# TensorE multiplies ones into an unused PSUM bank at eleven places of a two-block network kernel

## The chip, the cores and the metric

One NeuronCore of a Trainium2 chip runs the kernel. Its engines are TensorE (PE, with its weight loads listed as PEld), VectorE (DVE), ScalarE (ACT), GpSimd (POOL) and SyncE (SP), which here issues most of the DMAs. The metric is the time of one execution on the device in microseconds (us); lower is better.

## What is computed

256 tokens of width 1024 in float32 go through two blocks. The first has a depthwise convolution, an attention with a forget gate and 32 experts, of which each token takes 4. The second has two layers with a windowed attention and a retention in both directions, then a dense feed-forward in the first layer and 8 experts, 2 for each token, in the second. What matters here are the norms and the two routings, since the change stands around them:

```python
def rms_norm(x, g):
    y = xf * lax.rsqrt(jnp.mean(xf * xf, axis=-1, keepdims=True) + RMS_EPS)
    return (y * g)
def layer_norm_2(x, g, b):
    mu = jnp.mean(xf, axis=-1, keepdims=True)
    var = jnp.mean(jnp.square(xf - mu), axis=-1, keepdims=True)
    return ((xf - mu) * lax.rsqrt(var + LN_EPS)) * g + b

# routing of block 1 (block 2: 8 experts, top 2)
logits = (hf @ w_router + b_router)
top_v, top_e = lax.top_k(logits, TOP_K)
gates = jax.nn.softmax(top_v, axis=-1)
# each expert
hc = xi @ w1[e] + b1[e]
hm = (u + 1.0) * (g * jax.nn.sigmoid(SWIGLU_ALPHA * g))
y += gate * (hm @ w2[e] + b2[e])

# between the blocks and inside the second
x = rms_norm(x, final_g); x = layer_norm_2(x, ln_emb_g, ln_emb_b)
for layer in range(2):
    x = layer_norm_2(ALPHA * x + hybrid_mixer(x), ln1_g[layer], ln1_b[layer])
    x = layer_norm_2(ALPHA * x + ffn(x), ln2_g[layer], ln2_b[layer])
```

## The kernel before

Activations lie with the features on the partitions: X and H are 128 x 8 x 256 (feature within a tile, tile, token). Each engine runs a program written out by hand, in that order, and the engines wait for each other by counted semaphores; nothing is scheduled by a planner. Weights come by DMAs that SyncE issues in the order of use into a ring in SBUF; a slot is refilled when PE has used it.

**Sums over features.** Features lie on partitions, so a norm's sums are products with ONES, a 128x128 tile of ones, as the stationary side: each brings the sum over 128 features to all partitions. `squares` (L880) does it for the norm ahead of the first experts, `shift_sum` (L740) and `moments` (L748) for the layer norms, L1040 for the rms norm between the blocks. The layer norms first subtract an estimate of the mean (`shift_sum` on two tiles) and then take the sum and the sum of squares of the shifted values. DVE turns the sums into a factor (L1709 to L1752: a subtraction, ACT's square root, a reciprocal, the multiplication), ACT applies gain and bias pair of tiles by pair of tiles (L1476, L1395), and PE's next products wait for each pair.

**First products behind a norm.** `first_jobs` (L683) runs the first two weight slots of a stage pair by pair, with weights and activations in two float32r parts (WHI_D, WLO_D, XHI, XLO). POOL makes WLO_D (L400) for each slot from what ACT rounded (L396).

**Routing** (`route`, once for each expert stage). PE computes the logits (L903, moving part 32 or 8 columns), turns the tokens (L896), sums the mask of chosen experts (L909 to L912) and, in the first, turns the gates (L918). DVE computes the table of chunks from them; two small products (L922) bring it into a row. Then PE gathers the first chunk's tokens with a one-hot tile (L956 with 64 columns in the first stage, L1052 with 512 in the second), adds the bias products (L932, first stage only) and reads the number of chunks into a register (L936). The loop over chunks of 64 slots starts with L992 in the first stage and L1094 in the second. In each chunk PE also turns tiles and gathers for the next chunk (L1003, L956).

**The end.** PE turns the normed output (L1329), ACT and DVE copy it and SyncE stores it.

The line numbers here and in the prediction are those of this kernel.

Of the kernel before, what the change touches and what calls it, by code (L numbers as in the profile page):

```python
# [28 lines left out]
P = 128  # L29
# [110 lines left out]
def build_two_blocks(nc, A, out):  # L140
# [3 lines left out]
    with ctx:  # L144
        sems = {}

        def sem(name):
            if name not in sems:
                sems[name] = ctx.enter_context(nc.semaphore(name))
            return sems[name]  # L150
# [30 lines left out]
        ONES = sb("ONES", [P, P])  # L181
# [128 lines left out]
        def ps(b, n=512, p0=0, p1=P, c0=0):  # L310
            return PS[p0:p1, b, c0:c0 + n]
# [307 lines left out]
        def _(pe):  # L619
            norm = [0]  # L620

            def bank_free(job):
                if job >= 2:
                    e, c = job_evac[job - 2]
                    pe.wait_ge(sem("evac_" + e), c)
# [111 lines left out]
            def shift_sum(src, b):  # L737

                for k in range(2):
                    mm = pe.matmul(ps(b, T), ONES[:, :], src[:, k, :], start=(k == 0), stop=(k == 1))  # L740
                mm.then_inc(sem("norm_sum"), 1)

            def moments(src, squares, p, first, last, b1, b2):


                def total(bank, c0, x):
                    for k in (2 * p, 2 * p + 1):
                        mm = pe.matmul(ps(bank, T, c0=c0), ONES[:, :], x[:, k, :],  # L748
                                       start=(first and k == 2 * p), stop=(last and k == 2 * p + 1))
                    if last:  # L750
                        mm.then_inc(sem("norm_sum"), 1)

                norm[0] += 1
                if not last:
                    pe.wait_ge(sem("norm_in"), norm[0])
                total(b1, 0, src)
                pe.wait_ge(sem("norm_in"), norm[0])
                total(b2, T, squares)
# [116 lines left out]
            def squares(s):  # L875

                norm[0] += 1
                pe.wait_ge(sem("norm_in"), norm[0])
                for k in (2 * s, 2 * s + 1):
                    mm = pe.matmul(ps(4, T), ONES[:, :], SQV[:, k, :], start=(k == 0), stop=(k == KT - 1))  # L880
                mm.then_inc(sem("norm_sum"), 1)

            for s in range(4):
                feature_job(lins["w_out"], s, z(GC, GC + 8))
                if s:
                    squares(s - 1)
            squares(3)

            def route(m, x, wr, gather):

# [24 lines left out]
                if m is m1:  # L915
                    pe.wait_ge(sem("route_gates"), 1)
                    for a in range(2):
                        tr = pe.transpose(ps(1, P, c0=a * P), GATE4[:, a, :, :].rearrange("p r e -> p (r e)"), IDENT[:, :])  # L918
                    tr.then_inc(sem("gates_turned"), 1)
                pe.wait_ge(sem("route_table_cols"), m.nth)  # L920
                for j in range(2):
                    mm = pe.matmul(ps(3, P, 0, 1, 256 + j * P), TCOL[:, j:j + 1], IDENT[:, :], start=True, stop=True)  # L922
# [16 lines left out]
            def scatter_last(tag):  # L939


                for j in range(2):
                    for h in range(2):
                        c = (2 + j) * P
                        mm = pe.matmul(ps(4 + h, T, c0=j * T), YS1[64 * h:64 * h + 64, c:c + P], GT[64 * h:64 * h + 64, :],
                                       start=True, stop=True)
                mm.then_inc(sem(tag + "_scattered"), 1)

            def experts1():
# [81 lines left out]
                pe.wait_ge(sem("m1_ys_copied"), count + 1)  # L1031
                scatter(count, 0)
                scatter_last("m1")
                pe.wait_ge(sem("xw_ready"), 1)
                shift_sum(XW[:, 0:2, :], 1)
                for i, p in enumerate((0, 2, 1)):
                    moments(XW, XWSQ, p, i == 0, False, 3, 1)
                pe.wait_ge(sem("x_squared"), 1)
# [2 lines left out]
                mm.then_inc(sem("norm_sum"), 1)  # L1041
                pe.wait_ge(sem("xw_shifted"), 1)
                moments(XW, XWSQ, 3, False, True, 3, 1)

            def experts2():

# [100 lines left out]
                scatter_last("m2")  # L1147
                pe.wait_ge(sem("x_added"), 3)
                shift_sum(X, 3)
                for i, p in enumerate((0, 2, 1, 3)):  # L1150
                    if i == 3:
                        pe.wait_ge(sem("xw_shifted"), 2)
                    moments(X, H, p, i == 0, i == 3, 2, 3)
# [3 lines left out]
            def mixer2(l):  # L1157
# [112 lines left out]
                moments(X, H, 2, False, False, 5, 4)  # L1270
                pe.wait_ge(sem("evac_dve"), job_evac[lin.job0 + 3][1])
                moments(X, H, 3, False, True, 5, 4)

            mixer2(0)
            first_jobs(lins["ffn1"])
# [43 lines left out]
            for p in range(4):  # L1319
                if p == 3:  # L1320
                    pe.wait_ge(sem("x_added"), 2)
                moments(X, H, p, p == 0, p == 3, 5, 4)
            mixer2(1)
            experts2()
            for k in range(KT):
                if k % 2 == 0:
                    pe.wait_ge(sem("stream_x"), 16 + k // 2 + 1)
                for a in range(2):
                    tr = pe.transpose(ps(4 + 2 * a + k // 4, P, c0=(k % 4) * P), X[:, k, a * P:(a + 1) * P], IDENT[:, :])  # L1329
                    if k % 4 == 3:  # L1330
                        tr.then_inc(sem("out_turned"), 1)
# [1017 lines left out]
```

## Time and profile before

| | us |
|---|---|
| median of 3 runs (2408.94 to 2410.05) | 2409.09 |
| the profiled execution | 2402.67 |
| its span, first to last instruction | 2400.7 |
| PE busy in it | 2273.2 (95%) |
| VectorE, ScalarE, GpSimd busy | 735.9, 621.7, 385.2 |
| mean granted TensorE clock | 0.976 of full speed |

The stages by time in the span: norms, projections, convolution and attention of the first block until about 277; first routing until 306; 33 chunks of the first experts until 1270; the norms between the blocks until 1299; the first mixer until 1518; the dense feed-forward until 1724; the second mixer until 1948; second routing until 1972; 11 chunks of the second experts until 2375; the last norm and the output until 2400.7.

How to read it. Busy time counts pipelined products up to a modelled end, so that 95% does not say that PE runs at its peak. The granted clock is given as a share of 2.4 GHz: 1.00 is 2.4, 0.50 is 1.2 GHz, and a value between is the mean of a stretch in which it changed. A matmul on float32 data stands as two records in the trace. In a row of the timeline, the bracket at the end gives the idle time ahead and what ended it.

### The profile page before, as it was taken

Reading aid. Unit: us, or ns where it says so; the run is one execution under the profiler, and the core shown is the slowest. Engines: PE = TensorE matmul, PEld = TensorE weight load, DVE = VectorE, ACT = ScalarE, POOL = GpSimd, SP = SyncE. Lnnn points to the kernel's source line nnn. Section 1 sums busy time; section 2 is a strip of 40 time slices with the busy share of each in tenths; the row PEclk is TensorE's granted clock in tenths of the full one; section 3 lists DMA queues with packets and bytes.
Section 4 is the critical chain, followed back from the end, with each engine's and each line's share of the span. In section 5 each row is a group of like instructions: output and inputs, shape, how many; then the busy total and the mean of one; then the engine's idle time right before and its main releaser. Section 6 shows DMA issues by size and latency. Waiting matters only on the chain.

```text
span 2400.7 us, 34716 instructions
## 1 busy us (share of the span) xinstructions
PE 2273.2 (95%) x13090; PEld 1407.5 (59%) x13091; DVE 735.9 (31%) x1369; ACT 621.7 (26%) x901; POOL 385.2 (16%) x355
## 2 busy tenths in 40 slices
PE   5999899999999999999997999999999989999897
PEld 4887744444444444444446988899898863333333
DVE  6854322222222222222235234312314341111013
ACT  1143111111111111111214761443368011111111
POOL 1000000000000000000004741688486000000000
PEclk8999899999999999999998999999999989999999
DMA  9962389999999999989993433565454366999651
GB/s 371 370 233 101 95 341 418 418 418 417 418 417 418 417 418 417 418 341 414 418 393 106 158 106 105 163 190 180 119 176 124 122 249 260 362 405 396 278 234 72
DMA packets 226472, 688.61 MB, mean 287 GB/s; under 512 B 31386, under 2 KB 120418, under 8 KB 190562
## 3 DMA queue, kind: packets, MB, share of 16 engines
q1 hardware_dynamic: 221776, 685.82, 74.5%
q10 hardware_dynamic: 4626, 1.81, 0.3%
q8 instruction: 50, 0.82, 0.1%
q14 instruction: 20, 0.16, 0.0%
HBM read 686.53 MB, written 1.05 MB: 286 GB/s over the span
## 4 chain that ended last, share of the span: by engine, by line
PE 73%; DMA 10%; SPq 8%; DVE 4%; issue 1%; ACT 1%; ACTq 1%; POOL 0%; DVEq 0%; POOLq 0%
PE PS L992 16%; PE PS L651 12%; PE PS L662 11%; DMA RAW<-in_w_exp_in 9%; PE PS L1094 7%; SPq L453 6%; PE PS L1105 4%; PE PS L956 4%; PE PS L1287 3%; PE PS L975 2%; PE PS L706 1%; PE PS L748 1%; SPq L475 1%; PE PS L1003 1%; PE PS L1052 1%
## 5 line engine op out<-in xcount | busy, mean ns | idle before, releaser
L992 PE MATMUL PS<-RAW,Z 128*64 128x512 f32 x3168 | 713.7, 597 | 23.2 <-DMA RAW<-in_w_exp_in 23.2
L400 POOL TENSOR_TENSOR WLO_D<-W,WHI_D 128x512 fp32r<-128x512 f32 x284 | 361.8, 1310 | 1193.1 <-ACT WHI_D L396 1164.3
L992 PEld LDWEIGHTS PS<-RAW,Z 128*64 128x64 f32 x3168 | 213.7, 137 | 454.4 <-issue 376.7
L1094 PE MATMUL PS<-W,Z 128*64 128x512 f32 (+1 forms) x1056 | 212.8, 558 | 11.3 <-DMA W<-in_moe_w 10.6
L662 PE MATMUL PS<-Z,W 128*128 128x256 f32 x768 | 172.2, 385 | 2.1 <-DVE Z L1900 1.5
L396 ACT ACTIVATE WHI_D<-W 128x2048 fp32r<-128x2048 f32 x71 | 135.3, 1908 | 119.4 <-DMA W<-in_ffn_w 47.6
L1094 PEld LDWEIGHTS PS<-W,Z 128*64 128x64 f32 x1056 | 75.1, 137 | 149.1 <-issue 128.2
L662 PEld LDWEIGHTS PS<-Z,W 128*128 128x128 f32 x768 | 147.6, 193 | 25.2 <-DVE Z L1900 1.9
L956 PE MATMUL PS<-Z 128*128 128x64 f32 x1088 | 128.6, 278 | 0.0
L956 PEld LDWEIGHTS PS<-Z 128*128 128x128 f32 x1088 | 127.4, 196 | 0.3 <-issue 0.3
L2021 DVE TENSOR_TENSOR Z<-Z,PS 128x1024 f32<-128x1024 f32 x66 | 80.4, 1218 | 125.9 <-PE PS L975 125.9
L662 PE MATMUL PS<-H,W 128*128 128x256 f32 x512 | 116.1, 388 | 2.4 <-ACT Z L1432 2.4
L1515 ACT ACTIVATE Z<-PS 128x512 f32<-128x512 f32 x33 | 19.7, 597 | 367.1 <-PE PS L992 367.1
L651 PE MATMUL PS<-XHI,WHI_D 128*128 128x256 f32 x784 | 111.7, 285 | 1.4 <-POOL WLO_D L400 1.4
L1105 PE MATMUL PS<-W,Z 128*64 128x512 f32 x484 | 111.1, 599 | 0.0
L651 PE MATMUL PS<-XHI,WLO_D 128*128 128x256 f32 x784 | 110.1, 283 | 0.0
L651 PE MATMUL PS<-XLO,WHI_D 128*128 128x256 f32 x784 | 110.0, 283 | 0.0
L2047 DVE COPY Z<-PS 128x512 f32<-128x512 f32 x33 | 22.8, 692 | 280.0 <-PE PS L992 280.0
L662 PEld LDWEIGHTS PS<-H,W 128*128 128x128 f32 x512 | 98.8, 195 | 16.6 <-issue 2.9
L651 PEld LDWEIGHTS PS<-XHI,WHI_D 128*128 128x128 f32 x784 | 100.7, 191 | 3.1 <-POOL WLO_D L400 2.0
L651 PEld LDWEIGHTS PS<-XLO,WHI_D 128*128 128x128 f32 x784 | 101.1, 192 | 0.0
L651 PEld LDWEIGHTS PS<-XHI,WLO_D 128*128 128x128 f32 x784 | 101.1, 192 | 0.0
(384 smaller groups left out, 2333.8 us busy)
## 6 DMA issues: line engine op xcount, KB each, us to landing
RAW<-in_w_exp_in SPq DMA_DIRECT2D x256, 1024.0 KB, 19.3
RAW<-in_w_exp_out SPq DMA_DIRECT2D x128, 1024.0 KB, 21.8
W<-in_moe_w SPq DMA_DIRECT2D x128, 704.0 KB, 15.8
W<-in_w_in SPq DMA_DIRECT2D x52, 1024.0 KB, 5.9
W<-in_moe_w SPq DMA_DIRECT2D x40, 1024.0 KB, 16.1
W<-in_ffn_w SPq DMA_DIRECT2D x33, 1024.0 KB, 5.3
W<-in_w_ada SPq DMA_DIRECT2D x24, 1024.0 KB, 14.0
W<-in_w_out SPq DMA_DIRECT2D x12, 1024.0 KB, 5.1
```

Of the source, the lines that this page charges most:

```text
L396: eng.activation(hi, raw, ACT.Copy).then_inc(sem("dense_hi"), 1)
L400: i = eng.tensor_tensor(lo[:, c:c + 512], raw[:, c:c + 512], hi[:, c:c + 512].bitcast(F32), ALU.subtract)
L453: sp.dma_start(dst, src).then_inc(sem(f"raw{s}"), 16)
L651: mm = pe.matmul(ps(job % 2, T, c0=j * T), w[:, k, c:c + P], xp[:, k, :], start=(i == k == 0), stop=(i == 2 and k == KT - 1))
L662: mm = pe.matmul(ps(job % 2, T, c0=j * T), w[:, k, c:c + P], x[:, k, :], start=(k == 0), stop=(k == nk - 1))
L956: mm = pe.matmul(ps(2, HALF, c0=k * HALF), HT[:, a, k * P:(k + 1) * P], PICK[:, a, 0:HALF], start=(a == 0), stop=(a == 1))
L975: mm = pe.matmul(ps(6 + h, T, c0=j * T), YS1[64 * h:64 * h + 64, c:c + P], GT[64 * h:64 * h + 64, :], start=True, stop=True)
L992: mm = pe.matmul(ps(bank, 512, 64 * h, 64 * h + 64), x, w[:, c:c + 512], start=first, stop=final, skip_group_check=True)
L1094: mm = pe.matmul(o if b < 2 else o.rearrange("p (i n) -> p i n", i=2), X1[:, s, :], rhs, start=(s == 0), stop=(s == 7), skip_group_check=True)
L1105: mm = pe.matmul(ps(3, 512, 64 * h, 64 * h + 64), x, second2(j)[:, c:c + 512], start=(i == j == 0), stop=(j == 5), skip_group_check=True)
L1287: mm = pe.matmul(ps(j // 2, T, c0=(j % 2) * T), w[a][:, i, j * P:(j + 1) * P], x[:, i, :], start=(s == n == i == 0 and j % 2 == 0), stop=( ...
L2021: dve.tensor_tensor(o, o, PS[:, 6:8, :].rearrange("p h (k t) -> p h k t", k=2), ALU.add)\
```

## The change

A helper `busy(n, b)` is added to PE's program. It issues n float32 products with ONES as stationary and ONES, read four times, as 512 moving columns, into PSUM bank 2 or 0, a bank that nobody reads before it is written anew. The products wait for nothing and raise no semaphore. It is called at eleven places: behind the squares of the norm ahead of the first routing (5); in `route` behind the transposes and ahead of the wait for the table (2, in both routings); behind the last scatter of the first experts (5), behind `shift_sum` (2) and behind the moments (6) between the blocks; behind `shift_sum` of the last norm (2); behind the moments at the end of each mixer (5, twice) and of the feed-forward (5); and ahead of the output's transposes (5). No other instruction is changed.

```diff
+            def busy(n, b=2):
+                for _ in range(n):
+                    pe.matmul(ps(b).rearrange("p (a n) -> p a n", a=4), ONES[:, :],
+                              ONES[:, :].unsqueeze(1).broadcast_to([P, 4, P]), start=True, stop=True)
...
             squares(3)
+            busy(5)
...
                     tr.then_inc(sem("gates_turned"), 1)
+                busy(2)
                 pe.wait_ge(sem("route_table_cols"), m.nth)
...
                 scatter_last("m1")
+                busy(5)
                 pe.wait_ge(sem("xw_ready"), 1)
                 shift_sum(XW[:, 0:2, :], 1)
+                busy(2)
                 for i, p in enumerate((0, 2, 1)):
...
                 moments(XW, XWSQ, 3, False, True, 3, 1)
+                busy(6)
...
                 shift_sum(X, 3)
+                busy(2, 0)
...
                 moments(X, H, 3, False, True, 5, 4)
+                busy(5)
...
                 moments(X, H, p, p == 0, p == 3, 5, 4)
+            busy(5)
             mixer2(1)
             experts2()
+            busy(5, 0)
             for k in range(KT):
```

PE's order at the first routing before: the squares, the logits with the router's weights WR, the turned tokens, the mask sums, the gates, the table, the gather.

```order
L880 MATMUL PS<-SQ,ONES 128x256 x4
L903 MATMUL PS<-WR,H 128x32 x16
L896 MATMUL PS<-IDENT,H 128x128 x8
L909 MATMUL PS<-SQ,ONESB 128x32 x2
L910 MATMUL PS<-SQ,BEFOREB 128x32
L911 MATMUL PS<-SQ,ONESB 128x32
L912 MATMUL PS<-SQ,BEFOREB 128x32
L896 MATMUL PS<-IDENT,H 128x128 x8
L918 MATMUL PS<-IDENT,SQ 128x128 x2
L922 MATMUL PS<-IDENT,SQ 1x128 x2
```

The same place after, with line numbers of the changed kernel:

```order
L887 MATMUL PS<-SQ,ONES 128x256 x4
L626 MATMUL PS<-ONES 128x512 x5
L911 MATMUL PS<-WR,H 128x32 x16
L904 MATMUL PS<-IDENT,H 128x128 x8
L917 MATMUL PS<-SQ,ONESB 128x32 x2
L918 MATMUL PS<-SQ,BEFOREB 128x32
L919 MATMUL PS<-SQ,ONESB 128x32
L920 MATMUL PS<-SQ,BEFOREB 128x32
L904 MATMUL PS<-IDENT,H 128x128 x8
L926 MATMUL PS<-IDENT,SQ 128x128 x2
L626 MATMUL PS<-ONES 128x512 x2
L931 MATMUL PS<-IDENT,SQ 1x128 x2
```

Five products of 512 columns now stand between the squares and the logits, and two between the gates' transposes and the table's products.

PE's order from the last chunk of the first experts to the first mixer, before: transposes and scatters, the shift's sum, the moments, the first products with the split weights.

```order
L965 MATMUL PS<-IDENT,Z 128x128 x2
L971 ISA
L975 MATMUL PS<-Z,SQ 128x256 x4
L945 MATMUL PS<-Z,SQ 128x256 x4
L740 MATMUL PS<-Z,ONES 128x256 x2
L748 MATMUL PS<-Z,ONES 128x256 x12
L1040 MATMUL PS<-H,ONES 128x256 x8
L748 MATMUL PS<-Z,ONES 128x256 x4
L683 MATMUL PS<-XHI,WHI_D 128x256
```

The same after:

```order
L974 MATMUL PS<-IDENT,Z 128x128 x2
L980 ISA
L984 MATMUL PS<-Z,SQ 128x256 x4
L954 MATMUL PS<-Z,SQ 128x256 x4
L626 MATMUL PS<-ONES 128x512 x5
L747 MATMUL PS<-Z,ONES 128x256 x2
L626 MATMUL PS<-ONES 128x512 x2
L755 MATMUL PS<-Z,ONES 128x256 x12
L1051 MATMUL PS<-H,ONES 128x256 x8
L755 MATMUL PS<-Z,ONES 128x256 x4
L626 MATMUL PS<-ONES 128x512 x6
L690 MATMUL PS<-XHI,WHI_D 128x256
```

Five, two and six products now stand ahead of the shift's sum, ahead of the moments and ahead of the mixer's first products.

## Rows read from the trace of the kernel before

**Rows 1.** PE's waits: line, who released it, us, times, longest us.

```profile
PE PS L683 <- ACT XHI L1395: 15.4, 3, 5.4
...
PE PS L651 <- POOL WLO_D L400: 1.4, 1, 1.4
```

**Rows 2.** Windows, routing, loop: us; busy PE, PEld, DVE, ACT, POOL; clock, DMA, GB/s.

```profile
277.64:282.31 4.67, 0.00 (x0) 0.00 (x0) 4.04 (x6) 1.56 (x4) 0.00 (x0) 0.69 1.21 296
...
289.35:293.60 4.25, 3.95 (x23) 3.31 (x22) 3.56 (x20) 1.75 (x4) 0.00 (x0) 0.56 0.61 191
296.80:303.90 7.10, 7.10 (x37) 6.98 (x36) 0.87 (x4) 0.00 (x0) 0.00 (x0) 0.50 0.02 3
...
310.00:1256.00 946.00, 922.80 (x4992) 405.61 (x4992) 247.57 (x454) 171.63 (x225) 0.00 (x0) 1.00 1.01 412
```

**Rows 3.** Timeline of first routing: start, us, engine, operation, [idle before].

```profile
281.17 4.04 ACT L1476 ACTIVATE H<-H,MOD,GS 128x256 f32<-128x256 f32 x8 [2.54 <-DVE H L1922]
...
282.31 7.04 PE L903 MATMUL PS<-WR,H 128*128 128x32 f32 x32 [4.67 <-ACT H L1476]
...
293.20 0.38 PE L918 MATMUL PS<-IDENT,SQ 128*128 128x128 f32 x2
...
296.16 0.70 PE L922 MATMUL PS<-IDENT,SQ 128*1 128x128 f32 x4 [2.58 <-DVE SQ L1982]
...
296.80 7.09 PE L956 MATMUL PS<-Z 128*128 128x64 f32 x32
...
303.82 2.09 PE L932 MATMUL PS<-Z,W 32*128 32x256 f32 x16
...
305.84 4.09 PE L992 MATMUL PS<-RAW,Z 128*64 128x512 f32 x16
```

**Rows 4.** Timeline of PE in one round of the first expert loop.

```profile
350.76 3.68 PE L956 MATMUL PS<-Z 128*128 128x64 f32 x32
354.38 3.65 PE L992 MATMUL PS<-RAW,Z 128*64 128x512 f32 x16
```

**Rows 5.** Timeline of the norm between the two blocks.

```profile
1274.36 3.23 DVE L2073 SCALAR_TENSOR_TENSOR X<-PS,MOD,X 128x256 f32<-128x256 f32 x8
...
1276.23 2.07 PE L740 MATMUL PS<-Z,ONES 128*128 128x256 f32 x4 [4.99 <-ACT Z L1566]
...
1280.27 8.45 PE L748 MATMUL PS<-Z,ONES 128*128 128x256 f32 x24 [1.97 <-DVE Z L1731]
...
1292.01 1.89 PE L748 MATMUL PS<-Z,ONES 128*128 128x256 f32 x8
```

**Rows 6.** Windows around two norms, columns as in rows 2.

```profile
1276.23:1293.90 17.67, 15.70 (x52) 12.32 (x52) 7.77 (x15) 6.22 (x11) 0.00 (x0) 0.71 0.35 111
...
1299.27:1305.00 5.73, 5.73 (x32) 5.73 (x33) 3.52 (x6) 5.18 (x11) 2.94 (x3) 0.64 0.00 0
1518.10:1522.95 4.85, 0.00 (x0) 0.03 (x1) 4.73 (x8) 1.60 (x3) 0.00 (x0) 0.89 1.10 356
1522.95:1529.30 6.35, 6.35 (x32) 6.35 (x33) 3.85 (x7) 5.79 (x12) 0.00 (x0) 0.55 1.10 351
```

**Rows 7.** Timeline: ACT's fourth pair behind that first norm.

```profile
1302.02 1.09 ACT L1395 ACTIVATE XHI<-X,VEC 128x256 fp32r<-128x256 f32 x2 [0.23 <-DVE X L1752]
```

**Rows 8.** Timeline of the second routing and of the end.

```profile
1953.33 6.99 PE L903 MATMUL PS<-WR,X 128*128 128x8 f32 x32 [4.77 <-ACT X L1395]
...
1959.77 0.06 DVE L1936 MEMSET SQ<- 128x1 f32 x1
...
1966.18 1.01 PE L922 MATMUL PS<-IDENT,SQ 128*1 128x128 f32 x4 [1.90 <-DVE SQ L1982]
...
1967.12 2.88 PE L1052 MATMUL PS<-Z 128*64 128x512 f32 x8
...
2391.74 0.66 PE L1329 MATMUL PS<-IDENT,X 128*128 128x128 f32 x4 [4.77 <-ACT X L1395]
...
2395.72 1.12 PE L1329 MATMUL PS<-IDENT,X 128*128 128x128 f32 x4 [0.21 <-ACT X L1395]
```

## The prediction

> **What bounds the kernel now.** TensorE (PE) is busy for most of the span, so I first asked the list of waits where it stands [rows 1], then the windows and the timeline around each of those places [rows 2 to 8]. The reader should see three things. The waits are few and short: 15.4 us in three places ahead of L683, and single waits of 2 to 5 us ahead of L903, L922, L740, L748 and L1329. They sit where VectorE (DVE) and ScalarE (ACT) finish a norm or a routing table; PE has nothing real to do there. And behind them the granted clock reads 0.50, which is 1.2 GHz instead of 2.4: the gap 277.64 to 282.31 has mean 0.69, so the clock was high for 0.38 of 4.67 us, 1.8 us, then fell [rows 2]. The logits, the gather and the norm sums behind such gaps run at that level and are what the next engine waits for. So the waits cannot be won, but the half clock behind them can.
>
> **The price of one filler.** Each float32 product stands in the trace as two records. Four 256-column products with ONES at full clock take 1.89 us with their tail; the 24 records ahead end 0.16 us after the next ones begin, which is that tail [rows 5]. Without it they take 0.43 us each: 0.86 us for 512 columns, at most 0.94 with the tail in each. Full clock therefore gives 4.3 to 4.7 us for five, 5.2 to 5.7 for six, 1.7 to 1.9 for two, and twice that at 1.2 GHz. The gaps [rows 1, 2, 3, 5, 8] are 4.67 (L903, first), 2.58 (L922, first), 4.99 (L740), 1.97 (L748), up to 5.4 (L683), 4.77 (L903, second), 1.90 (L922, second), 4.77 (L1329). At 0.86 every filler ends 0.1 to 0.9 us before its gap does; I take it, because products that stand in a row show no tail between them. Nothing but PE's next step is queued behind a filler: the semaphores that DVE and ACT wait for are raised by the real product ahead of it. Its cost is zero by that cover; with the upper length up to 0.3 us at the six.
>
> **First routing, before the experts.** ACT gives h in four pairs; the last is there at 281.17 + 4.04 = 285.2 [rows 3]. The logits are 32 records in 7.04 us, bound by their loads; the gather, also 128x128 loads with narrow moving parts, does 32 records in 3.68 us in the expert loop at clock 1.00 [rows 2, 4], 0.11 us each. At full clock the last pair's eight records end at 285.35 + 0.86 = 286.2 instead of 289.35: **3.1 us**. DVE's chain to the table columns follows them and moves as a whole. Then come two fillers: the gates' transposes end at 293.58, L922 waits until 296.16, both 3.1 earlier, and 1.7 fits into 2.58. Next the gather: 7.09 us at 0.50 against 3.68 gives 3.4. The bias products behind it give nothing, since PE's queue is reading registers for the same 2.0 us (303.82 to 305.84, during L932 [rows 3]). The first products of the loop take 4.09 us for 16 records, 3.65 at full clock [rows 3, 4]: 0.4. Together **3.8 us** more. The expert stage starts on PE's first products and nothing is late for it: its first weights are in SBUF (DMA share 0.02 at 296.80 to 303.90).
>
> Does that survive the expert stage, which moves 412 GB/s [rows 2] and so goes at DMA's pace? I think so: SyncE issues the second expert's weights only when PE has used the first's, so stream and stage move together.
>
> A rule to weigh here. At 289.35 to 293.60 PE did mainly transposes and the mean clock is 0.56: it was low for 3.7 us and rose before the end [rows 2]; the table products at 296.16 then began after 2.58 us of idle. The Trainium skill ("TensorE: Matmul & The Clock Gate", Part 4: PE-mode transpose) says that transposes do not count as PE activity for the clock. By it the two fillers behind the transposes could start at half clock and take 3.4 us in a gap of 2.58. The rise seen here speaks against it in this kernel. With the rule, 0.9 us of the 3.8 would go, and the gather's 3.4 would depend on the two fillers alone.
>
> **The norm between the blocks.** After the five, shift_sum's four records run at full clock, but DVE is busy with L2073 until 1277.59 and its next step ran at 1278.34, so only 0.75 is won [rows 5]. Then 48 records (L748 x24, L1040 x16, L748 x8) stand from 1280.27 to 1293.90; 8 records in 1.72 us make that 10.3 instead of 13.5 without the tail: 3.1. Sum **3.85 us**. Cross-check: mean clock 0.71 over 1276.23 to 1293.90 means 10.2 us at half clock, of which some 2 are idle [rows 6].
>
> **First products behind a norm (L683).** 32 records took 5.73 us at mean clock 0.64 and 6.35 at 0.55 [rows 6]; the two equations give 0.21 us a record at half and 0.13 at full clock. At full clock ACT's pairs bind: the fourth is there at 1303.11 [rows 7], plus 0.14 and eight records of 0.13, 1304.3 against 1305.0: **0.7 us**. The same pace behind 1522.95 ends at 1528.0 against 1529.3: **1.3 us**. In the third place PE soon waits 1.4 us for POOL's L400 [rows 1], whose work hangs on ACT and not on PE: **0**.
>
> **Second routing.** The logits could end 2.2 us earlier, but DVE is in its own memsets until 1959.83 and used them at 1960.43: 0.5 [rows 8]. The two fillers (gap 1.90) may begin at half clock here, behind an 8-column stretch and transposes: 3.4 us, 1.0 late after the 0.5. Against it stands the gather L1052 at full clock, 2.88 to 1.94. Bounds -0.1 and +1.9 (fillers at full clock throughout); I take **1.2**, for a clock that rises during the fillers, as it did under dense products in every other place. **Second norm:** its clock is high already, nothing. **End:** four transposes 1.12 against 0.66 us [rows 8]: **0.4**.
>
> Sum: 3.1 + 3.8 + 3.85 + 0.7 + 1.3 + 0 + 1.2 + 0.4 = 14.4 us. The profiled execution took 2402.67 us (span 2400.7), which would become 2388.3. The median of the runs shown is 6.4 us above the profiled one; I subtract from the median: 2409.1 - 14.4 = **2394.7 us**, own range 2391 to 2399.
>
> **Rivals.** *1. The clock falls again in the narrow stretches.* Logits of 32 and 8 columns and a 64-column gather do not lift a low clock: it reads 0.50 through 7.1 us of gather [rows 2]. If they cannot hold a high one either, and it falls 1.8 us after the last filler as in rows 2 (283.6), the first logits win 1.35 us; the two fillers run at half clock, 3.4 in 2.58, and lose 0.9; the gather wins nothing; the second routing loses 0.5. The norms keep 5.85 and the end 0.4. Sum 6.2: **2402.9**. For it: those 7.1 us. Against: the loop has the same gather, 3.68 us long, every time round, and its 946 us read 1.00 [rows 2, 4]. By the skill's rule on transposes this is where it would end too.
>
> *2. Slower: the fillers do not keep the clock.* If products of ones leave the clock as it was, each runs partly at half clock. With the fall 1.8 us into a gap, five take 1.8 + 2 x 2.5 = 6.8 us: 2.1 over the gap at the first logits, 1.9 before ffn1, 2.1 at the second logits; six take 8.5, 3.1 over; two take 3.4, 1.5 over in each of two gaps. That is up to 12.2; falls as late as in the gap before 1522.95 (mean 0.89, so 3.8 us in [rows 6]) halve it. Price +9: **2418**. It decides once the filler's length at the granted clock passes the gap. Against: sums with ONES alone lifted the clock between 1276.23 and 1293.90.
>
> *3. The expert stage gives the routing's gain back.* If the stream and not PE set its end, 6.9 us are lost and 7.5 stay: **2401.6**. Against: DMA stands idle before it starts.
>
> *4. No effect*, the clock edges just elsewhere: **2409**. *5. More:* the second routing at its upper bound (0.7 more), L932 at full clock (1.0 more if the register reading shortens), and, since runs without the profiler take 6.4 us longer, perhaps longer stretches at half clock there for the fillers to win back: 17 to 20 us, **2390**.
>
> **How the numbers follow.** Forecast 0.52; rival 1 0.22; rival 2 0.06; rival 3 0.06; rival 4 0.05; rival 5 0.09. The range 2389 to 2403.5 holds the forecast, most of rival 1, rival 3 and half of rival 5, about 0.8. A measurement of this kernel can tell some 0.2%, 4.8 us, from no change, so faster means below 2404.3: 0.52 + 0.18 + 0.06 + 0.09 = 0.85. Same: 0.04 + 0.05 = 0.09. Slower: 0.06.
>
> **What would show it.** In the changed profile the granted clock reads 1.00 in the gaps before L903, L740, L748 and L683 and behind them; the first logits take some 4 us, limited by ACT, and the gather 3.7 instead of 7.1; the 48 norm records take 10.3; the first loop product starts 6.5 us earlier relative to the last squares. PE's waits at these places shrink to under 1 us, and none becomes zero with DVE or ACT waiting for PE. Wrong would be: a filler that ends after its gap, a clock of 0.50 during the logits or the gather, or a longer expert stage.

## The result

| | before | after |
|---|---|---|
| median, us | 2408.81 (6 runs, 2405.69 to 2410.05) | 2390.78 (6 runs, 2387.62 to 2399.13) |
| ratio, 95% interval | | 0.9934, 0.9923 to 0.9945 |
| profiled execution, us | 2402.67 | 2392.87 |
| its span, us | 2400.7 | 2390.9 |
| mean granted clock | 0.976 | 0.988 |

The change makes the kernel faster by 0.66%, some 16 us by the ratio (13.2 to 18.5 us), and the two medians lie 18.0 us apart; the forecast was 14.4 us and 2394.7 us. A second set of runs of the same changed kernel (e0) gives 0.9945, some 13 us. The two profiled executions differ by 9.8 us only, and a later section says how far that is explained.

### The profile page after: what moved, and what is told of

Its sections match the earlier page's. It is cut to its first block, busy times and chain, and to the rows that moved or that the text cites. A ratio compares the mean times of both kernels' runs of the same rounds, so it can differ in the third digit from the quotient of the medians.

```text
span 2390.9 us, 34892 instructions
## 1 busy us (share of the span) xinstructions
PE 2296.2 (96%) x13178; PEld 1409.0 (59%) x13179; DVE 735.8 (31%) x1369; ACT 621.6 (26%) x901; POOL 385.0 (16%) x355
## 4 chain that ended last, share of the span: by engine, by line
PE 72%; DMA 11%; SPq 8%; DVE 4%; issue 1%; ACT 1%; ACTq 1%; POOL 0%; DVEq 0%; POOLq 0%
PE PS L1001 16%; PE PS L658 12%; PE PS L669 11%; DMA RAW<-in_w_exp_in 10%; PE PS L1106 7%; SPq L453 6%; PE PS L1117 4%; PE PS L965 4%; PE PS L1301 3%; PE PS L984 2%; SPq L475 2%; DMA W<-in_moe_w 2%; PE PS L713 1%; PE PS L755 1%; PE PS L1012 1%
## 5 line engine op out<-in xcount | busy, mean ns | idle before, releaser
L1001 PE MATMUL PS<-RAW,Z 128*64 128x512 f32 x3168 | 713.2, 597 | 24.3 <-DMA RAW<-in_w_exp_in 23.4
L1001 PEld LDWEIGHTS PS<-RAW,Z 128*64 128x64 f32 x3168 | 213.7, 136 | 454.7 <-issue 376.6
L669 PE MATMUL PS<-Z,W 128*128 128x256 f32 x768 | 173.2, 387 | 1.5 <-DVE Z L1916 1.5
L669 PEld LDWEIGHTS PS<-Z,W 128*128 128x128 f32 x768 | 148.4, 194 | 25.0 <-DVE Z L1916 1.9
L965 PE MATMUL PS<-Z 128*128 128x64 f32 x1088 | 125.3, 273 | 0.0
L965 PEld LDWEIGHTS PS<-Z 128*128 128x128 f32 x1088 | 124.2, 192 | 0.2 <-issue 0.2
L669 PE MATMUL PS<-H,W 128*128 128x256 f32 x512 | 116.2, 388 | 2.7 <-ACT Z L1448 2.7
L669 PEld LDWEIGHTS PS<-H,W 128*128 128x128 f32 x512 | 99.0, 195 | 16.9 <-issue 3.3
## 6 DMA issues: line engine op xcount, KB each, us to landing
W<-in_w_ada SPq DMA_DIRECT2D x24, 1024.0 KB, 13.5
```

The source lines that it names most:

```text
L669: mm = pe.matmul(ps(job % 2, T, c0=j * T), w[:, k, c:c + P], x[:, k, :], start=(k == 0), stop=(k == nk - 1))
L965: mm = pe.matmul(ps(2, HALF, c0=k * HALF), HT[:, a, k * P:(k + 1) * P], PICK[:, a, 0:HALF], start=(a == 0), stop=(a == 1))
L1001: mm = pe.matmul(ps(bank, 512, 64 * h, 64 * h + 64), x, w[:, c:c + 512], start=first, stop=final, skip_group_check=True)
```

## The profile after

First the first routing on PE, against [rows 3]: start, duration, engine, line, operation, [idle before]. L626 is the helper `busy`, L911 the logits, L931 the table, L965 the gather, L941 the bias products, L1001 the loop's products.

```profile
277.62 4.45 PE L626 MATMUL PS<-ONES 128*128 128x512 f32 x10
282.46 4.05 PE L911 MATMUL PS<-WR,H 128*128 128x32 f32 x32 [0.38 <-ACT H L1492]
...
290.32 1.88 PE L626 MATMUL PS<-ONES 128*128 128x512 f32 x4
293.32 0.60 PE L931 MATMUL PS<-IDENT,SQ 128*1 128x128 f32 x4 [1.12 <-DVE SQ L1998]
293.85 3.79 PE L965 MATMUL PS<-Z 128*128 128x64 f32 x32
297.56 1.15 PE L941 MATMUL PS<-Z,W 32*128 32x256 f32 x16
299.57 3.65 PE L1001 MATMUL PS<-RAW,Z 128*64 128x512 f32 x16 [0.87 <-issue]
```

The five products take 4.45 us and end 0.38 us before ACT's last step ahead of the logits, so they delay nothing. The 32 logits records take 4.05 us instead of 7.04 and the gather 3.79 instead of 7.09. The bias products halve too, but the loop still starts 2.0 us after they begin: 0.87 us is "issue", the register being read.

Windows of the same place (us, PE busy, granted clock, DMA share, GB/s), against [rows 2]:

```profile
277.78:282.46 4.68, 4.30 (x12) 1.00 1.21 296
282.46:286.32 3.86, 3.86 (x32) 1.00 1.35 217
...
286.32:289.70 3.38, 3.10 (x20) 0.50 1.27 244
289.70:293.85 4.15, 3.03 (x16) 1.00 0.55 176
...
293.85:299.57 5.72, 4.86 (x49) 1.00 0.01 1
```

The gap, the logits and the gather read 1.00. One stretch of 3.4 us at 0.50 is left, right behind the logits. It lies on turns and mask sums, where DVE sets the pace: from the first turn to the table PE takes 7.0 us before and after.

The norm between the blocks, against [rows 5]; L747 is the shift's sum, L755 and L1051 are the 48 sums, L690 the mixer's first product:

```profile
1264.64 4.56 PE L626 MATMUL PS<-ONES 128*128 128x512 f32 x10
1269.71 1.13 PE L747 MATMUL PS<-Z,ONES 128*128 128x256 f32 x4 [0.51 <-ACT Z L1582]
1270.68 1.88 PE L626 MATMUL PS<-ONES 128*128 128x512 f32 x4
1272.90 5.45 PE L755 MATMUL PS<-Z,ONES 128*128 128x256 f32 x24 [0.34 <-DVE Z L1747]
1278.18 3.62 PE L1051 MATMUL PS<-H,ONES 128*128 128x256 f32 x16
1281.64 1.89 PE L755 MATMUL PS<-Z,ONES 128*128 128x256 f32 x8
1283.36 5.31 PE L626 MATMUL PS<-ONES 128*128 128x512 f32 x12
1288.90 0.36 PE L690 MATMUL PS<-XHI,WHI_D 128*128 128x256 f32 x1 [0.23 <-ACT XHI L1411]
```

All three gaps are covered with 0.2 to 0.5 us left over. From 1272.90 to 1283.4 the 48 sums take 10.5 us; they were spread over 13.6.

The second routing and the end, against [rows 8]; L1064 is the gather, L1345 the output's transposes:

```profile
1945.70 3.58 PE L911 MATMUL PS<-WR,X 128*128 128x8 f32 x16 [0.17 <-ACT X L1411]
...
1953.21 2.99 PE L626 MATMUL PS<-ONES 128*128 128x512 f32 x4
1956.13 0.60 PE L931 MATMUL PS<-IDENT,SQ 128*1 128x128 f32 x4
1956.65 1.95 PE L1064 MATMUL PS<-Z 128*64 128x512 f32 x8
...
2385.91 1.11 PE L1345 MATMUL PS<-IDENT,X 128*128 128x128 f32 x4 [0.67 <-ACT X L1411]
```

Here the clock did fall during the eight-column logits, and the two products run mostly at half clock: 2.99 us. DVE's last step ahead of the table (L1998) starts at 1955.11 and takes 0.15 us, so the table's products start 0.87 us late. In return the clock is high again for the gather.

PE's waits, the places of [rows 1] among them (line, releaser, us, times, longest):

```profile
PE PS L658 <- POOL WLO_D L400: 2.0, 1, 2.0
...
PE PS L690 <- ACT XHI L1411: 1.7, 3, 0.9
```

The 15.4 us of waits before the first products are 1.7, and the wait for POOL grew from 1.4 to 2.0.

## Where the time went

I laid the two traces side by side by the starts of the same instructions. A plus is time won by the change.

| stretch | before | after | won |
|---|---|---|---|
| last squares to logits | 4.67 | 4.68 | 0 |
| logits to turns | 6.85 | 3.86 | +3.0 |
| gather to first loop product | 9.04 | 5.72 | +3.3 |
| first experts | 970.39 | 970.14 | +0.25 |
| shift's sum to mixer's first product | 23.04 | 19.19 | +3.85 |
| its two slots, the same before the feed-forward | 9.59, 10.29 | 8.80, 8.79 | +0.8, +1.5 |
| first mixer | 210.25 | 211.05 | -0.8 |
| behind the wait for POOL, second mixer | 2.97 | 4.46 | -1.5 |
| logits to gather, gather to loop, second routing | 13.79, 4.99 | 13.61, 4.06 | +0.2, +0.9 |
| second experts | 404.51 | 406.10 | -1.6 |
| last norm, output's transposes | 15.12, 3.98 | 15.12, 3.98 | 0, 0 |

Stretches of some tenths and less are left out. The places with products give 13.5 us together, and three stretches without any take 3.9 back. The 0.8 us won in the first mixer's two slots is gone again at the mixer's end: from its first product to the feed-forward's PE takes 223.7 us before and after.

## The experiments

Each kernel starts from the changed one. e2, e3, e4 and e5 ran on one chip with the kernel before, e0, e1, e6 and e7 on another, e8 to e10 on one again. A ratio is always to the kernel before, with its 95% interval.

**Which place gives what.** `e2_first_routing` keeps only the products of the first routing:

```diff
-                busy(2)
+                if m is m1:
+                    busy(2)
...
                 scatter_last("m1")
-                busy(5)
                 pe.wait_ge(sem("xw_ready"), 1)
```

The other calls from there to the end are gone in the same way. Expected: 

> Only the five products ahead of the first routing's logits and the two ahead of its table are kept. Theory (the products hold the clock, and everything behind moves with it): the logits take about 4 us instead of 7, the gather 3.8 instead of 7.1, the loop's first product starts 6.4 us earlier, the expert stage keeps that, and the kernel is 6.4 to 6.9 us faster than before, ratio 0.9972. Rival (the first expert stage runs at DMA's pace and gives the gain back): the loop starts 6.4 us earlier, but the stage is longer by as much, ratio 1.000.

Measured: 2401.12 us against 2407.08, 0.9977 (0.9967 to 0.9986): 0.23%, 5.5 us.

`e3_norms` keeps the five, two and six between the blocks and the five behind the first mixer:

```diff
             squares(3)
-            busy(5)
...
-                busy(2)
                 pe.wait_ge(sem("route_table_cols"), m.nth)
...
                 moments(X, H, 3, False, True, 5, 4)
-                busy(5)
+                if l == 0:
+                    busy(5)
```

The other calls are gone too. Expected: 

> Only the products around the norm between the blocks (5, 2, 6) and the five behind the first mixer are kept. Theory: 3.85 us from the norm's sums, 0.7 and 1.3 from the first products behind the two norms, 5.9 us in all, ratio 0.9975. Rival (what is won behind a norm is lost in the mixer, where PE then waits for POOL, ACT or DVE, as 0.8 of it was in the changed kernel's trace): 3.9 to 4.5 us, ratio 0.9983.

Measured: 2403.37, 0.9981 (0.9972 to 0.9990): 0.19%, 4.6 us. The interval holds the theory's 5.9 and the rival's 3.9 to 4.5; the trace sides with the rival on one term. From the mixer's first product to the feed-forward's it has 223.3 us, against 223.4 and 223.6 in e2 and e5 without the products, so the 0.7 us won at its start is not there at its end. From the feed-forward's first product to the second mixer's it has 205.4 against 206.7 and 206.8, so the 1.3 us is kept.

`e5_second_routing` keeps the five behind the second mixer and the two in the second routing:

```diff
-                busy(2)
+                if m is m2:
+                    busy(2)
...
-                busy(5)
+                if l == 1:
+                    busy(5)
```

Here too the other calls are gone. Expected: 

> Only the five products ahead of the second routing's logits and the two ahead of its table are kept. Theory: the clock falls in the 8-column logits, the two products begin at half clock and end up to 1 us late, but lift it for the gather; 1.1 us gained, ratio 0.9995. Rival (the late products cost as much as the gather wins): 0, ratio 1.000; the second expert stage lost 1.6 us in the changed kernel's trace, and if that comes from this place and not from chance, the kernel is 0.5 us slower and its loop from first product to last is again about 406 us instead of 404.5.

Measured: 2403.14, 0.9987 (0.9978 to 0.9996): 0.13%, 3.1 us. The second experts took 403.1 us here, so the longer stage of which the rival spoke (406) does not show with these products.

`e4_without_three` is the changed kernel without three calls for which I had forecast nothing or 0.4 us:

```diff
-                busy(2, 0)
...
-            busy(5)
             mixer2(1)
             experts2()
-            busy(5, 0)
```

Expected: 

> The changed kernel without the products in the last norm (2), ahead of the second mixer (5) and ahead of the output (5). Theory (no gain was foreseen at the first two, 0.4 us at the third): the same as the changed kernel within 0.5 us, ratio to before 0.9934. Rival: ahead of the second mixer the products only made PE arrive earlier at its wait for POOL, the wait grew to 2.0 us, the clock fell behind it and 1.6 us were lost; without them the kernel is 1 to 1.5 us faster than the changed one, ratio 0.9929.

Measured: 2394.56, 0.9950 (0.9936 to 0.9963).

What follows: the first routing gives most, and the three parts add up to 0.55% where the whole gives 0.55 and 0.66%, so no loss between them shows (each part is known to 0.1% only); the first experts' stage hands the routing's gain on (their stage takes 970.1 us after, 970.4 before, 969.8 with the first routing's products alone). Rival 3 is out. The three calls left out in e4 cannot be told from nothing by the time. The trace tells one thing of them. In e4 the gap before the output reads 0.99 and what stands behind it 0.50:

```profile
2374.40:2379.34 4.94, 0.18 (x1) 0.99 0.00 0
2379.34:2385.00 5.66, 4.46 (x16) 0.50 0.06 23
...
2367.76 1.63 PE L755 MATMUL PS<-H,ONES 128*128 128x256 f32 x4
2369.23 1.03 PE L755 MATMUL PS<-X,ONES 128*128 128x256 f32 x4
```

Four records of the last norm's sums took 1.63 us here, 1.03 after the clock had risen. Of the profiled executions without 512-column products at that norm (before, e1, e2, e3, e4, e5) three show such a fall, with 16.6 to 16.8 us from the shift's sum to the output instead of 15.12; of the seven with them none does.

**The same kernel again.** `e0_changed_again` is the changed kernel, unedited. Expected: 

> The changed kernel again, beside the three below. Every theory expects the ratio to before that it had, 0.9934 within its interval (0.9923 to 0.9945). Where the clock falls in the narrow stretches may differ from its first trace: the mixers and the second routing show it.

Measured: 2394.26 against 2408.45, 0.9945 (0.9932 to 0.9958), some 13 us. Its profile shows how executions of one kernel differ:

```profile
283.82 4.86 PE L911 MATMUL PS<-WR,H 128*128 128x32 f32 x32 [0.38 <-ACT H L1492]
...
283.82:285.50 1.68, 1.68 (x14) 1.00 1.35 218
285.50:288.50 3.00, 3.00 (x20) 0.70 1.35 217
```

The clock fell inside the 32-column logits, which took 4.67 us to the turns and not 3.86, although the five products ahead had run at 1.00. But the second mixer has no fall behind POOL's wait (2.97 instead of 4.46 us), with the same wait of 2.0 us, and the second experts take 404.0 us.

**Is it the clock, or only that PE is not idle?** `e1_narrow` puts four products of 8 columns where one of 512 stood:

```diff
-                for _ in range(n):
-                    pe.matmul(ps(b).rearrange("p (a n) -> p a n", a=4), ONES[:, :],
-                              ONES[:, :].unsqueeze(1).broadcast_to([P, 4, P]), start=True, stop=True)
+                for _ in range(4 * n):
+                    pe.matmul(ps(b, 8), ONES[:, :], ONES[:, 0:8], start=True, stop=True)
```

Expected: 

> Each product of 512 columns is replaced by four products of 8 columns with the same stationary ones. At full clock such a product costs two weight loads of 0.108 us, so five of the old ones and twenty of these both take 4.3 us. Theory (what helps is that dense products keep the clock high): the clock falls in or right behind the narrow ones as in the gaps before, 40 records take up to 6.8 us instead of 4.3, the logits, the gather and the norm sums run at half clock as before; no gain, and up to 12 us slower than before, ratio 1.000 to 1.005, granted clock of the run about 0.975. Rival (any work in PE's queue helps, by keeping it fed or by its weights): as the changed kernel, ratio 0.993.

Measured: 2416.47, 1.0037 (1.0025 to 1.0050), 9 us slower than the kernel before.

```profile
280.79 6.69 PE L626 MATMUL PS<-ONES 128*128 128x8 f32 x40
287.32 7.01 PE L910 MATMUL PS<-WR,H 128*128 128x32 f32 x32
...
280.19:284.00 3.81, 3.81 (x29) 0.84 1.09 345
284.00:290.00 6.00, 6.00 (x30) 0.50 1.34 220
```

PE is busy without a break, and the clock falls all the same: the 40 records take 6.69 us in a gap of 4.67, the logits 1.7 us late and at half clock. So the gain comes through the clock, and a busy PE is not enough for it. This is also rival 2's mechanism, shown with products that do not hold the clock, at nearly its price (2416 against 2418).

**More of them.** `e6_more` adds a product of 256 columns behind each of the first three pairs of the second logits, and two of 512 in the second layer's first products, where PE waits for POOL:

```diff
+                    if m is m2 and k in (1, 3, 5):
+                        half()
...
+                if l == 1:
+                    busy(2, 6)
```

Expected: 

> The changed kernel, plus one product of 256 columns behind each of the first three pairs of the second routing's logits (gap there 0.47 us, the product 0.43) and two of 512 behind the first products of the second mixer, where PE waits 2.0 us for POOL. Theory: the clock stays high through the logits, the table's two products end in their gap, the second routing takes 12.8 us from logits to gather instead of 13.6, and the 1.5 us that the fallen clock cost behind POOL's wait are gone: 1 to 2 us faster than the changed kernel, ratio 0.9928. Rival (the added products end late and push the logits): the second routing is longer by up to 0.5 us, ratio 0.9936.

Measured: 2394.93, 0.9954 (0.9938 to 0.9970): no gain over the changed kernel. Locally it works a little (logits to gather 13.19 us instead of 13.61, and 2.96 behind POOL's wait), but the clock still fell in the logits: records 1.50 and 1.72 us long per pair instead of some 1.0. The second experts took 408.5 us.

What the two products saved behind POOL's wait was lost again before the mixer's end. From its first product to the second logits the second mixer took 225.1 us in e6, as in the changed kernel's first profile (225.1), and 223.6 in e0. The loss lies at the output's products: the ones on 16 partitions (L1268 of the changed kernel) and the 128 records behind them. Their windows in e0 and in e10, where the second mixer is as long as in e6:

```profile
1883.69:1916.89 33.20, 33.20 (x146) 0.95 0.69 267
1891.10:1925.81 34.71, 34.71 (x146) 0.90 0.67 255
```

The clock was low there for 3.4 us in e0 and for 6.8 us in e6, e8, e9 and e10.

`e7_start` adds seven at the very start:

```diff
             x_squares()
+            busy(7)
```

Expected: 

> The changed kernel, plus seven products of 512 columns (6.0 us) behind the first norm's sums at the start, where PE waits 6.8 us for VectorE and runs at half clock for the 13 us behind it. Theory: the sixteen one-column products take 3.5 us instead of 7.0 and the first projections start up to 3.5 us earlier, but weights for them come at 370 GB/s with the queues full until 120 us, so of the 3.5 to 6 us between 0 and 3 are left: ratio 0.9925 to 0.9934. Rival (PE and not DMA sets this stretch): 5 us faster than the changed kernel, ratio 0.991.

Measured: 2395.68, 0.9952 (0.9940 to 0.9965). PE's first projections, L669, of this kernel:

```profile
40.89 15.65 PE L669 MATMUL PS<-H,W 128*128 128x256 f32 x64
61.52 4.77 PE L669 MATMUL PS<-H,W 128*128 128x256 f32 x14 [4.98 <-ACT Z L1449]
```

and of the changed one:

```profile
43.53 15.96 PE L669 MATMUL PS<-H,W 128*128 128x256 f32 x64
62.23 6.07 PE L669 MATMUL PS<-H,W 128*128 128x256 f32 x27 [2.73 <-ACT Z L1448]
```

PE is 2.6 us earlier and then waits 2.3 us longer for ACT; 0.7 us is left behind it. At the end of the stage nothing of it can be seen: the squares ahead of the first logits end at 282.2 us, in the twelve other profiles at 277.6 to 281.0. The start goes at another engine's pace, and there the clock is worth nothing.

**How many, and where.** `e8_longer` passes the cover of two gaps on purpose:

```diff
-            busy(5)
+            busy(8)
...
-                busy(6)
+                busy(8)
```

(before the first logits, and before the mixer's first product). Expected: 

> The changed kernel with eight products instead of five before the first routing's logits and eight instead of six before the first mixer of the second block. Each product takes 0.44 us at full clock and 0.86 us at half, and in the changed kernel's profile ten records (five products) took 4.45 us, twelve (six) 5.31 us. Theory (a product beyond its gap costs its whole duration, and buys nothing once the clock is held): the wait of 4.67 us before the logits is passed by 8 x 0.86 - 4.67 = 2.2 us if the products run as the five did, less if the last three run at full clock (0.44 each, 1.3 us less: 0.9 us late); the six before the mixer end 0.2 us before the squares' result, so two more cost 0.9 to 1.7 us there. Sum 1.8 to 3.9 us over the changed kernel (2394.3): 2396 to 2398. Rival (a longer row of products keeps the clock up for longer and saves the stretches of half clock that are left, as the one in the first logits that some executions show): logits at 3.6 us for all 32 and the time no more than the changed kernel's.

Measured: 2395.73, 0.9939 (0.9923 to 0.9956). The time does not show the price; the trace does:

```profile
279.00 7.03 PE L626 MATMUL PS<-ONES 128*128 128x512 f32 x16
285.87 3.65 PE L911 MATMUL PS<-WR,H 128*128 128x32 f32 x32
...
1286.34 7.03 PE L626 MATMUL PS<-ONES 128*128 128x512 f32 x16
1292.80 0.69 PE L690 MATMUL PS<-XHI,WHI_D 128*128 128x256 f32 x1
```

Eight products take 7.03 us, 0.86 each and the tail; the logits start 2.0 us late and then need 3.49 us to the turns instead of 3.86, because ACT's pairs all lie ready. At the mixer 0.9 us is lost and 0.7 regained in the same way. Net 1.9 us, at the lower end of what was expected, and too little to show in the median of four runs. The clock held through all the logits here, as the rival said; but it did so with five products too, in the changed kernel's profile, e6 and e10, so one profile does not speak for eight.

`e9_fewer` halves every call, rounded up:

```diff
-                for _ in range(n):
+                for _ in range((n + 1) // 2):
```

Expected: 

> The changed kernel with three products in place of five, one in place of two and three in place of six, everywhere. Theory (what matters is how long TensorE stands without products, and 2 us of it do no harm, as the gaps of 1.9 to 2.6 us do in the changed kernel where a gap is only partly filled): the time of the changed kernel within 2 us, 2393 to 2396. Rival (the full clock needs the whole gap filled): the clock falls again in the first routing and the norm between the blocks as it does before the change, worth 6.6 and 3.9 us in their profiles, so 2400 to 2405. The granted clock of the logits, the gather and the mixer's squares tells which, place by place.

Measured: 2394.73, 0.9945 (0.9929 to 0.9962), the same as the changed kernel.

```profile
279.26 2.74 PE L626 MATMUL PS<-ONES 128*128 128x512 f32 x6
284.10 4.67 PE L911 MATMUL PS<-WR,H 128*128 128x32 f32 x32 [2.10 <-ACT H L1492]
...
1285.59 2.74 PE L626 MATMUL PS<-ONES 128*128 128x512 f32 x6
1291.12 0.55 PE L690 MATMUL PS<-XHI,WHI_D 128*128 128x256 f32 x1 [2.80 <-ACT XHI L1411]
...
296.10:301.88 5.78, 4.86 (x50) 1.00 0.02 4
...
1291.12:1300.23 9.11, 9.11 (x64) 0.83 0.01 2
```

With 2.1 us of idle left the logits run as in e0, and the gather at 1.00. With 2.8 us left before the mixer the clock fell once, for 3.4 us, and cost 0.3. The gap need not be filled to the end.

`e10_no_two` takes away the two products ahead of the table, in both routings:

```diff
-                busy(2)
                 pe.wait_ge(sem("route_table_cols"), m.nth)
```

Expected: 

> The changed kernel without the two products between the turns of the logits and the table's transposes, in both routings. Theory (the gap of 2.6 us behind the short turns, with transposes on both sides, lets the clock fall again by the gather): gather to first loop product back at 7.5 to 9.0 us from 5.7, in the second routing gather to first loop product 5 to 6.3 us from 4.1, together 2.7 to 5.5 us: 2397 to 2400. Rival (the five products before the logits and the logits themselves hold it through, and the two do nothing): both stretches as in the changed kernel, 2394 to 2395.

Measured: 2398.85, 0.9954 (0.9936 to 0.9971). The interval overlaps with the others, so the trace is read:

```profile
296.50 0.92 PE L930 MATMUL PS<-IDENT,SQ 128*1 128x128 f32 x4 [2.68 <-DVE SQ L1997]
297.35 7.09 PE L964 MATMUL PS<-Z 128*128 128x64 f32 x32
...
289.54:293.82 4.28, 3.79 (x25) 0.60 1.23 266
293.82:296.50 2.68, 0.00 (x0) 1.00 0.51 162
297.35:306.39 9.04, 9.04 (x49) 0.50 0.00 1
```

Gather to first loop product is 9.04 us again, exactly as before the change. From logits to first loop product that makes 3.6 us in the first routing. In the second, gather to loop takes 5.79 us instead of 4.06, but the gather starts 0.4 us earlier without the late products, which leaves 1.3 us. Together the two calls of two products are worth 4.9 us. The gather's whole gain hangs on them: the five ahead of the logits do not give it by themselves. Whether the two would do it without the five no run tests in the first routing. The gap itself read 1.00 throughout; the fall came at its end.

## Why the prediction was right

The direction and the mechanism came as forecast, and so did the time: 2390.8 us is 3.9 under the forecast of 2394.7 and just under its own range of 2391 to 2399, but inside the wide one of 2389 to 2403.5, and e0 gives 2394.3. The sum came out partly by terms that cancel, as the steps show:

- **Price and cover of a filler:** 0.86 us each (4.45 for five, 5.31 for six, 1.88 for two); in the changed kernel's profile every call but one ends 0.2 to 1.1 us before its gap does. Right. The exception is the two in the second routing, for which 3.4 us and 1.0 late had been allowed: 2.99 and 0.87.
- **First logits, 3.1:** 3.0 in this profile, but the clock fell inside the logits in e0, e2, e4, e7 and e9, five of the nine profiles with 512-column products ahead of them, and there 2.2 to 2.4 was won. This is rival 1 in part: 32 columns do not surely hold the clock. The term was 0.8 too large for about half of the executions.
- **Gather and first loop products, 3.8:** 3.3 up to the loop and 0.4 in it. Right, the 2.0 us of register reading included. Rival 1 said that the gather would win nothing; e10 shows what that would have looked like, and that the two products prevent it.
- **The stage keeps the gain:** right, above.
- **Norm between the blocks, 3.85:** 3.85 between the two profiles; 3.2 and 3.6 against e2 and e5, where the same stretch without products took 22.40 and 22.81 us and not 23.04.
- **First products, 0.7, 1.3 and 0:** 0.8, 1.5, and 0 in the third place itself. The 1.5 is kept: from the feed-forward's first product to the second mixer's all profiles with 512-column products in between take 205.4 us (e9, with fewer, 206.0), those without 206.7 to 206.9. The 0.8 is not: from its first product to the feed-forward's the first mixer took 222.8 to 225.3 us, mean 223.8, in the nine profiles with such products ahead of it, and 223.4 to 223.7 in the three with none. And the third place, put at nothing, seems to cost. PE now comes earlier to POOL's wait and waits 2.0 instead of 1.4 us; in two of the five profiles with that wait (after and e7; not in e0, e8 and e10) the clock fell there, mean 0.62 over 4.46 us, and took 1.5 us. In e6, e8, e9 and e10 about as much went at the output's products instead. So the second mixer took 225.1 to 225.2 us in six of the seven profiles with 512-column products ahead of it (e0: 223.6) and 223.5 in four of the five with none (before, e2, e3, e5; e4: 224.4). The prediction costed this edit at nothing without asking what the earlier start does to the clock behind it; that the edit is the cause is suggested by these counts and not shown.
- **Second routing, 1.2:** 1.1 between the two profiles; too small against other executions. Without products the stretch from gather to loop took 6.27 us in e2 and e3, and 4.99 in the profile on which the prediction rests; with them 4.06 in all but e10. Against 6.27 that is 2.4 us, and e5 measures 3.1 (1.0 to 5.3).
- **Last norm, 0:** 0 between the two profiles, up to 1.7 us in three of six executions without the products. The premise "its clock is high already" took one execution for all.
- **End, 0.4:** 0. ACT hands over a pair every 1.33 us, so the length of the first three groups of transposes does not count, and the fourth ran at half clock in both. At full clock it would have given nothing either: in e0, e8 and e10 the fourth took 0.66 us and ended 0.46 earlier, and the end still came 9.0 us after the first group, as in all other profiles. The output's four stores land one behind the other, some 0.65 us apart, and the last of them 0.41 us before the end, with the fourth group at either clock.

The sum of 14.4 lies between the 16 and the 13 us of the two sets of runs, with three terms too large (first logits and end, up to 1.2 together, and the first mixer's 0.7), one too small (second routing, by up to 1.2), and the second mixer's loss of about 1.5 left out. That these nearly cancel is luck.

The first set's 2390.8 us lies next to rival 5's 2390, but that does not make rival 5 right: it wanted 17 to 20 us, and e0's interval ends at 16.4. Of its three terms the second routing's came. The bias products' 1.0 did not, since the loop still starts 2.0 us after they begin. The third, longer low stretches outside the profiled execution, is small: the 44 other runs of the kernel before on record have a mean clock of 0.971 to 0.977, with medians of 0.974 to 0.976 on the three chips, against 0.976 in the profiled one.

**Why the two profiles differ by 9.8 only.** The profiled execution before was 6.1 us faster than its median, the one after 2.1 us slower. The low stretches move between executions of one kernel; that behind POOL's wait is one place, others are the first mixer (210.2 to 212.9 us over all the profiles, 210.25 before and 211.05 after) and above all the second experts, 403.1 to 409.4 us (before 404.5, after 406.1, e0 and e9 404.0, e8 408.5). Of the first mixer's 0.8 us the counts above say that it is mostly not kept; why is open. The 1.6 us of the second experts could not be tied to the change: with products somewhere in the kernel the stage took 403.1 to 409.4 us, in the profile before 404.5. It stays open. Subtracting from the median, and not from the profiled time, brought the forecast nearer: from the profiled time it would have been 2388.3.

**The rule on transposes.** Between 289.54 and 293.82 e10 has turns, mask sums and gates only. The mean clock over it reads 0.60: it was low for 3.4 us and then rose, and the gap behind reads 1.00. The Trainium skill ("TensorE: Matmul & The Clock Gate", Part 4: PE-mode transpose) says that a transpose in the engine's transpose mode does not count as busy time of PE in the same way and that the full clock does not engage for it. These float32 transposes, with some narrow mask sums between them, were followed by a rise before the next products in five profiles (before, after, e5, e6 and e10), where the trace does not agree (they stand in it as MATMUL with IDENT, and it does not say whether they ran in that mode). In e3 they were not, where the clock stayed at 0.50 from 283.3 on through turns, table and gather.

By the rule the two products of the first routing would have started at half clock and taken 3.4 us. Their start at half clock came true in five profiles (e0, e2, e4, e7 and e8), where the clock was low from the logits or the turns on; but it rose 0.5 to 0.9 us after they began, and they took 2.1 to 2.3 us and still fitted their gap. In the changed kernel's first profile and in e6 they began at 1.00 and took 1.88.

## What to carry to other kernels

Look for short steps that run at half clock behind a wait of PE's and that another engine waits for; there, wide products without a reader, placed in the wait, give back half of that step, and nothing where another engine sets the pace (e7, the output). They need not fill the gap: half of them gave the same time here (e9), and two between narrow steps carried a third of the gain (e10), but narrow ones are worse than none (e1). Cost such a change against several executions, since the low stretches wander, and ask of each wait that grows whether the clock survives it. And follow a gain to the end of its stage: the 0.8 us won at the first mixer's start was not there at its end.

## What was not expected of the hardware

- A busy PE does not by itself keep the clock: 40 records of 8 columns back to back fell to 0.50 (e1), and during the 32 records of 32 columns it fell in five profiles of nine; the 32 of 64 columns (the gather) kept it in every profile with products right ahead.
- The clock of a gap does not tell that of the work behind it: e10's gap of 2.68 us read 1.00, and the gather behind it 0.50; in e4 a gap of 4.94 us read 0.99 and what followed 0.50.
- The time at half clock was 118 us in the profile before, 57 after, and 77 in e9, whose time was the same as that of the changed kernel: what counts is which work a low stretch meets.
